# Exponentials ahead of the tanh, half of ada_w behind the first projection, a reordered last layer norm and one product fewer

## What is computed

```
mod = silu(c) @ ada_w + ada_b            # shift1, scale1, gate1, shift2, scale2, gate2
u = x * (1 + scale1) + shift1
q, k, v, lru_x, lru_gate, gate_a, gate_b = split(u @ w_in)
y_a = sliding_window_attention(q, k, v)   # window 128, sinks, relative bias
y_b = rg_lru(lru_x) * gelu(lru_gate)      # conv, gates, linear scan over the tokens
y = sigmoid(gate_a) * y_a + sigmoid(gate_b) * y_b
x = layer_norm(alpha * x + gate1 * (y @ w_out))
u = x * (1 + scale2) + shift2
f = grouped_moe(u)                        # router: one of 4 groups, 2 of its 4 experts
x = layer_norm(alpha * x + gate2 * f)
```

## Time and profile before

| | us |
|---|---|
| median of three runs | 744.32 |
| lowest, highest | 742.08, 747.95 |
| the profiled execution | 745.63 |
| its span | 743.4 |
| TensorE busy | 655.1 (88%) |
| VectorE, ScalarE, GpSimd busy | 341.4, 232.2, 99.9 |

### The profile page before, as it was taken

How to read it: one execution, slowest core, us unless ns; L and a number is a source line. 1 busy time by engine, 2 the same in 40 slices (tenths; PEclk the granted TensorE clock), 3 DMA queues, 4 the chain that set the end, 5 groups by cost and what they waited for, 6 DMA issues and landing times.

```text
span 743.4 us, 15575 instructions
## 1 busy us (share of the span) xinstructions
PE 655.1 (88%) x6007; PEld 427.3 (57%) x6008; DVE 341.4 (46%) x660; ACT 232.2 (31%) x483; POOL 99.9 (13%) x185
## 2 busy tenths in 40 slices
PE   3698999998999799999999849799999999999910
PEld 0366666676776577777788634355555555555500
DVE  0455445266778777566766585211111111111127
ACT  0424434458655455546510401011111111111112
POOL 0220000020000000000000013122222222222240
PEclk9999999999999899999999859899999999999965
DMA  9999766284221331222597977999999999992156
GB/s 330 373 304 309 255 226 227 86 308 138 85 59 56 86 86 56 77 66 87 180 409 307 386 302 286 416 419 419 419 418 419 418 419 418 419 418 88 42 162 199
DMA packets 83884, 189.16 MB, mean 254 GB/s; under 512 B 7388, under 2 KB 60092, under 8 KB 68488
## 3 DMA queue, kind: packets, MB, share of 16 engines
q1 hardware_dynamic: 67664, 148.66, 53.1%
q0 software_dynamic: 7376, 32.26, 12.6%
q10 hardware_dynamic: 8808, 7.76, 3.1%
HBM read 174.58 MB, written 14.07 MB: 254 GB/s over the span
## 4 chain that ended last, share of the span: by engine, by line
PE 66%; DMA 12%; DVE 8%; ACT 7%; issue 4%; SPq 1%; POOL 1%; ACTq 0%; POOLq 0%; DVEq 0%
PE psum L1565 18%; PE psum L1576 9%; PE psum L1355 7%; PE psum L1356 6%; PE psum L1357 6%; DMA raw<-in_w_in_dram 4%; DMA x_sb<-in_x_dram 3%; DMA wu<-in_moe_w_up_dram 3%; PE psum L1476 2%; PE psum L1478 2%; PE psum L1477 2%; PE psum L1312 2%; PE psum L1547 2%; PE psum L1554 2%; ACT ssb L775 2%
## 5 line engine op out<-in xcount | busy, mean ns | idle before, releaser
L1565 PE MATMUL psum<-wu,xs 128*32 128x256 f32 x1280 | 148.2, 384 | 0.3 <-issue 0.3
L1355 PE MATMUL psum<-uh,whi 128*128 128x512 f32 x336 | 138.8, 413 | 3.6 <-DVE wlo L918 3.6
L1356 PE MATMUL psum<-ul,whi 128*128 128x512 f32 x336 | 132.1, 393 | 0.0
L1357 PE MATMUL psum<-uh,wlo 128*128 128x512 f32 x336 | 131.8, 392 | 0.0
L1565 PE MATMUL psum<-wg,xs 128*32 128x256 f32 x832 | 95.0, 381 | 0.5 <-ACT xs L843 0.5
L918 DVE TENSOR_TENSOR wlo<-raw,whi 128x1024 fp32r<-128x1024 f32 x42 | 51.4, 1223 | 73.9 <-ACT whi L654 73.5
L837 ACT ACTIVATE hsil<-psum 64x256 f32<-64x256 f32 x40 | 15.0, 375 | 223.6 <-PE psum L1565 223.6
L1232 DVE TENSOR_TENSOR h_sb<-psum,hsil 64x256 f32<-64x256 f32 x40 | 17.1, 428 | 139.8 <-ACT hsil L837 139.8
L1355 PEld LDWEIGHTS psum<-uh,whi 128*128 128x128 f32 x336 | 63.8, 190 | 25.5 <-issue 7.7
L1576 PE MATMUL psum<-wd,hT 128*32 128x256 f32 x1280 | 77.4, 382 | 0.6 <-DVE hT L1238 0.6
L1565 PEld LDWEIGHTS psum<-wu,xs 128*32 128x32 f32 x1280 | 71.9, 111 | 1.3 <-issue 0.7
(11 more groups left out here) (265 smaller groups left out, 871.0 us busy)
## 6 DMA issues: line engine op xcount, KB each, us to landing
wu<-in_moe_w_up_dram SPq DMA_DIRECT2D x32, 1024.0 KB, 18.8
wd<-in_moe_w_down_dram SPq DMA_DIRECT2D x32, 1024.0 KB
wg<-in_moe_w_gate_dram SPq DMA_DIRECT2D x22, 1024.0 KB, 12.9
raw<-in_w_in_dram SPq DMA_DIRECT2D x42, 512.0 KB, 3.9
ada<-in_ada_w_dram POOLq DMA_DIRECT2D x16, 1024.0 KB, 5.8
wg_later<-in_moe_w_gate_dram SPq DMA_DIRECT2D x10, 1024.0 KB, 19.5
ada<-in_ada_w_dram SPq DMA_DIRECT2D x8, 1024.0 KB, 14.7
y_d<-ysb ACTq DMA_DIRECT2D x160, 32.0 KB
```

Of the source, the lines that this page charges most:

```text
L1355: mmul(bank[s % 2], h[:, k, :], uh[:, k, :], start=(k == 0), stop=False)
L1356: mmul(bank[s % 2], h[:, k, :], ul[:, k, :], start=False, stop=False)
L1357: ins = mmul(bank[s % 2], l[:, k, :], uh[:, k, :], start=False, stop=(k == KT - 1))
L1565: ins = mmul(psum[32 * g:32 * g + 32, 0, 0:256], xs[:, k % 2, k // 2, :], (gate, wgu[slot][1])[g // 2][:, k, (g % 2) * 256:(g % 2) * 256 + ...
```

## The change

Four edits. The exponentials of a unit and the tanh change places within ScalarE's step. POOL waits for the first projection (`proj_ps` at 1) before it issues anything but `flip`, and the products of ada_w move to steps 3, 3, 4, 4, 5, 6, 6, 7, 8, 8, 9, 9, 10, 11, 11, 12. In the last layer norm ScalarE takes the moments and the square root of tile 3 ahead of the columns of tile 1, and the exponential that brings in the table moves behind the columns of tile 3. `warm()` makes one product instead of two.

```diff
--- before.py
+++ after.py
@@ -59,7 +59,7 @@
 
 NA2 = 16
 A2_BUFS = 3
-A2_AT = [2 + (11 * n) // NA2 for n in range(NA2)]
+A2_AT = [3 + (10 * n) // NA2 for n in range(NA2)]
 
 
 
@@ -546,6 +546,7 @@
             pool.dma_start(sinkt[:, :], attn_sink[0].partition_broadcast(P)).then_inc(S["pool_in"], 16)
             pool.wait_ge(S["u_lo"], 1)
             pool.dma_start(flip[:, :], consts[:, C_FLIP:C_FLIP + P]).then_inc(flip_in, 16)
+            pool.wait_ge(S["proj_ps"], 1)
             for n in range(NA2):
                 j, half = n // 2, n % 2
                 if n == A2_BUFS:
@@ -761,10 +762,6 @@
                     act.wait_ge(S["o_ps"], n + 1)
                     A(q_sb[:, 2 * hg:2 * hg + 2, blk_ * P:(blk_ + 1) * P],
                       bank[6][:, 0:256].rearrange("p (i q) -> p i q", i=2), ACT.Copy).then_inc(S["ya_done"], 1)
-                i = s - (AT["lg", 0] + 1)
-                if 0 <= i < KT:
-                    act.wait_ge(S["g_arg"], i + 1)
-                    A(gt[i % 2][:, :], gt[i % 2][:, :], ACT.Tanh, scale=math.sqrt(2 / math.pi)).then_inc(S["g_tanh"], 1)
                 n = UNIT_AT.get(s - 1)
                 if n is not None:
                     act.wait_ge(S["logit_done"], n + 1)
@@ -775,6 +772,10 @@
                             A(v, v, ACT.Exp, bias=negm[:, n % 4, 2 * a + b:2 * a + b + 1],
                               accum_out=rsum[:, n % 4, 2 * a + b:2 * a + b + 1]).then_inc(S["exp_done"], 1)
                     A(sm[:, n % 4, :], sm[:, n % 4, :], ACT.Exp).then_inc(S["exp_done"], 1)
+                i = s - (AT["lg", 0] + 1)
+                if 0 <= i < KT:
+                    act.wait_ge(S["g_arg"], i + 1)
+                    A(gt[i % 2][:, :], gt[i % 2][:, :], ACT.Tanh, scale=math.sqrt(2 / math.pi)).then_inc(S["g_tanh"], 1)
                 i = s - (AT["ga", 0] + 2)
                 if 0 <= i < KT:
                     act.wait_ge(S["y_done"], i + 1)
@@ -807,7 +808,6 @@
                 store_u2(t)
             u2_columns(0)
             logit_parts(0)
-            u2_columns(1)
             last = NT - 1
             act.wait_ge(S["x1_sum"], 1)
             A(fsum[:, last, 1:2], fsum[:, last, 0:1], ACT.Copy, scale=-1.0 / D).then_inc(S["x1_mean"], 1)
@@ -816,12 +816,13 @@
                 .then_inc(S["x1_mean"], 1)
             act.wait_ge(S["x1_mean"], 2)
             A(rstd[:, last:NT], fsum[:, last, 2:3], ACT.Sqrt, bias=epst[:, 0:1], scale=1.0 / D).then_inc(S["ln_sqrt"], 1)
-            A(tiny[:, 1, :], tiny[:, 1, :], ACT.Exp).then_inc(S["exp_table"], 1)
+            u2_columns(1)
             logit_parts(1)
             u2_columns(2)
             logit_parts(2)
             store_u2(NT - 1)
             u2_columns(NT - 1)
+            A(tiny[:, 1, :], tiny[:, 1, :], ACT.Exp).then_inc(S["exp_table"], 1)
             logit_parts(NT - 1)
             act.wait_ge(S["rt_exp_in"], 1)
             A(sc[:, :, :], lg_[:, :, :], ACT.Exp).then_inc(S["rt_exp"], 1)
@@ -1536,7 +1537,7 @@
             def warm():
 
                 pe.wait_ge(gu_in[0][0], 32)
-                for k in range(2):
+                for k in range(1):
                     mmul(bank[4], ident, wg_first[:, k, :], start=True, stop=True)
 
             warm()
```

## The result

| | before | after |
|---|---|---|
| median of the runs, us | 743.20 (739.67 to 747.95, 4 runs) | 732.89 (732.22 to 733.91, 4 runs) |
| profiled execution, us | 745.63 | 732.22 |
| its span, us | 743.4 | 730.0 |
| mean granted clock | 0.942 | 0.961 |

The ratio is 0.9869, with a 95% interval of 0.9841 to 0.9897: 9.7 us less (7.6 to 11.8). The changed kernel ran again beside three others later, and gave 732.85 us and 0.9859 (0.9840 to 0.9879). The two profiled executions differ by 13.4 us. That is more than the interval of the timed difference holds, and where the rest comes from is the main lesson of this study.

What follows compares the result with a forecast made beforehand. The prediction took the kernel to be bound by TensorE, two thirds of the chain, with its stalls and half clock. It summed 745.63 - 4.5 - 7.3 - 0.6 - 0.7 = 732.5 (731.2 from the median), said 732, range 726 to 739.

Steps and rivals of the forecast that it cites:

- A: Projection 3: holding ada_w back lands tile 3 of w_in in time; gain 4.5 us, bounds -4.5 and +1.9.
- B: GeLU steps, 200 to 260 us: exponentials ahead of the tanh cut waits and half clock; gain 7.3 us, bounds 3.5 to 10.0.
- D: Ahead of the experts: one warm product fewer starts gate_up earlier; gain 0.7 us, bounds -1.8 and +0.4.
- stall three: TensorE's 4.45 us wait for ScalarE before the product of 251.44; that product 5.9 us earlier, 1.2 us of stall left.
- Stall two: TensorE's 0.97 us wait for ScalarE in the GeLU steps; 0.8 us of it to be covered.
- C: Last layer norm: earlier moments bring tile 3's transposes forward; gain 0.5 to 0.6 us, bounds +0.3 and -2.2.
- fits by 0.0: Last layer norm: 1.28 us table load plus 0.21 us exponential fit ScalarE's 1.52 us wait for the last router part.
- A fails: Rival at tile 3 of w_in: the stall stays and only moves; 737 to 739 us, chance 0.14.
- B gives half: Rival in steps 20 to 25: small delays on VectorE or TensorE appear again; 736 us, chance 0.10.
- The experts absorb it: Rival, experts' blocks: loads tied to time turn the earlier start into a wait at block 25; 743 us, chance 0.06.
- The tanh never became late: Rival in the GeLU steps: the tanh behind the exponentials becomes late and holds VectorE's GeLU; 749 us, chance 0.05.
- The clock rival: Shorter warm-up: clock back only at 451.9, gate_up gives up 2.2 us, D becomes +0.4; 733.6 us, chance 0.05.

Runs made afterwards that it cites:

- ln: Kernel before with only the reordering of the last layer norm on ScalarE; 742.59 us against 742.64, ratio 0.9993.
- warm1: Kernel before with only one unread warm product instead of two; 741.83 us against 742.64, ratio 0.9993.
- hold: Kernel before with only POOL's wait for the first projection and the products of ada_w moved to step 3 and later; 740.26 us against 742.64, ratio 0.9976.
- at_only: Kernel before with only the new order of the ada_w products, without POOL's held-back issue; 743.51 us against 743.17, ratio 0.9999.
- swap: Kernel before with only the exponentials put ahead of the tanh; 735.43 us against 742.64, ratio 0.9920.
- late fill: Changed kernel with GpSimd's zero fill of y_d held until after projection 27; 729.62 us, ratio 0.9804.
- late_again: Changed kernel with the zero fill of y_d behind projection 27, run once more; 731.02 us beside 732.85 for the changed kernel, ratio 0.9842.

## Why the prediction was right, and which terms were not

Predicted were 732.0 us (726 to 739) and faster; 732.9 were measured. The time is right, and the mechanisms of A and B are those that the traces show; D's too, but its gain is too small to be told from nothing. The size of the change isn't: the working takes 13.1 us off the profiled execution, 12.3 off the median of three runs, and the timed difference is 9.7 (7.6 to 11.8). Two errors cancelled, so that 732.0 came so near 732.9 is in part luck.

- **The base.** The sum started at 745.63 us. Over 25 later runs before stood at 742.64 us. The prediction noted that its execution lay 1.3 us above the median shown; it lies 2.4 to 3.0 us above the medians of more runs. With exact terms it would have come out too high by that.
- **A, 4.5 us.** The place, the cause and the landing held: tile 3 landed at 44.9 us, at the early end of 44 to 54, and q1 had its queue alone until q0's first large packets. The trace pair gives 4.90 us. But the term took the stall and 1.6 us of half clock from one execution as fixed. Only two of five traces with the old wait and the old order (before, ln) have a half clock in projection 3, and warm1's stall is 0.68 us. Over the traces A is worth 2.8 us, timed 1.7 to 1.8. The terms behind it held: tile 4 had landed by 54.56 us (near 57 was said, 59.5 needed), and no wait followed.
- **B, 7.3 us.** Alone 5.9 us (4.2 to 7.6), by the traces 6.1 on average and 6.5 in the pair. Its steps held: stall three at 1.11 to 1.84 us (1.2 said), no half clock behind it, the next product's wait 0.94 to 0.96 (1.4 said). Stall two was to be almost covered; in six of the nine kernels with B 0.55 to 0.58 us of it are left. Two of the five traces without B, hold and at_only, have half as much half clock behind stall three as before and are 1.3 to 1.5 us shorter for it; spread over five traces, that is 0.5 us of the 1.2 that the term had too much.
- **C, 0.6 us.** Timed 0.5, which can't be told from nothing. The gain of 0.5 us up to the transposes of tile 3 came. The step that failed is that the table load "fits by 0.0" into the 1.52 us in which ScalarE waits for the last router part: that row was taken at half clock, and at full clock the gap is 0.54 us. There the load and its exponential end at 413.92, the copy that the router's sum waits for is 0.9 us late, and C costs 0.34 us instead (after against swap): the bound of +0.3, not the value. The 2.0 us in the pair of profiles is the clock's. The Trainium skill (ScalarE: Activation LUTs, What ACT_TABLE_LOAD costs) gives 2.66 us for every switch to a different set; by that C would have been +0.8. The trace has 1.28 us and 0.01 to the next instruction, and the measurement decides.
- **D, 0.7 us.** 0.6 over the traces, 0.5 timed alone (1.6 less to 0.6 more); the column without D alone spreads over 2.0 us, so neither is clear of nothing. One product is 1.71 us, not 1.8. The clock came back 5.7 us after the product's start in after, within the 4.2 to 6.2 used; in the other six traces with one call it took 5.6 to 6.0 us in three and 3.8 to 4.0 in three. The Trainium skill (TensorE: Matmul & The Clock Gate, Part 1: The HAM clock gate) calls the half rate the default that activity releases; the traces agree in so far as the clock of block 0 is late with one call and back with two. That the next step, no call at all, cost nothing (731.08 against 731.02) doesn't bear out more than that.
- **Rivals.** "A fails" is what at_only shows for the order alone, not for A. "B gives half" is excluded by swap. "The experts absorb it" is excluded by the constant lead from block 5 to 24; the 0.9 us lost behind block 5 in the pair came from a bandwidth wait that before and ln have too. (The DMA engines are full from 465 us on; from 446 to 465 has 286 GB/s.) The tanh never became late, but in the last of its five steps behind exponentials it came within 0.03 us of it: its input was ready at 252.54 and it began at 252.57. In the other four ScalarE had 1.40 us or more to spare. The clock rival's +0.4 for D is not borne out by the averages.
- **The pair of profiles adds up**: 4.90 (A) + 0.13 + 6.50 (B) - 0.87 (loads of x for the first norm landed later) + 1.99 (router) + 1.62 (to block 5) - 0.86 (to the end) = 13.41 us. Of these, averages over the traces leave 2.8 (A) + 6.1 (B) + 0.6 (router) + 0.6 (D) = 10.1, in keeping with the timed 9.7. The router's 0.6 (25.92 us without C, 25.35 with it, late fill apart) is by the pairs above the clock's, not C's, and the columns to the second product, to the router and to the end are left out. The four parts timed alone sum to 8.7 us.

Not settled: why the clock falls at one of two places in the router part; what A and D are worth beyond their intervals (0 to 3.5 us, and 1.6 less to 0.6 more); and whether the version with the late fill is faster by over 1 us.

## What to carry to other kernels

Read a gain that hangs on a stall plus a half-clock stretch from several executions, or count the clock's share apart: here some 1.5 of the 2.9 us by which A and B were put too high (1.6 us in two of five traces, 1.4 us in three of five) were half clock of one execution. A stall on a fixed landing also swallows whatever came late ahead of it, so taking it away is worth less than its length whenever the work ahead varies. When a load of small packets is late, look first for large ones from another queue beside it, and delay those; the stall went at both places where that was tried here. When a step is moved into a gap that was read from a row at half clock, price the gap at full clock too.

## What the runs showed of the hardware that was not expected

- A load of 512-byte packets on q1 hardly moves while q0 has large ones under way: 0.13 MB in 4 us beside 1.30 MB, 1.15 MB in the same 4 us with q0 nearly empty. The earlier trace rows lists almost as many packets of q0 (264) as of q1 (262), though 75 of q0's are under 512 bytes; so in that stretch the two shared more by packets than by bytes. Whether the size of q0's packets is the cause, and not only that they were there, was not tested. The same at 150 us: 13.6 us beside the zero fill, 4.5 to 5.4 without. SyncE's own issue stream shows it too: the eight small writes of mod_d took it 10.23 us to issue beside the fill and 2.53 us without.
- One program has its half-clock stretches at different places from one execution to the next. The first projection begins at 35.4 to 36.6 us in nine traces and at 37.3 to 38.6 in five.
- A stretch of half clock on TensorE can cost almost nothing where waits for ScalarE follow: after has one such stretch at 181.7 that late_again lacks (from the second to the third product with v 15.70 against 14.12 us), but stands only 2.05 us for ScalarE behind it where late_again stands 3.3, and the distance from the second to the eighth product is 70.69 against 70.45 us.
